# Mixers stage of a hybrid decoder step: scan output made feature by token

## The reference, cut to what matters

```python
cum = jnp.cumsum(dtc * a.reshape(g, r), axis=2)
seg = cum[:, :, :, None] - cum[:, :, None, :]
decay = jnp.exp(jnp.where(causal, seg, -jnp.inf))
cb = jnp.einsum('bcign,bcjgn->bcijg', cc, bc)
y_diag = jnp.einsum('bcijgr,bcjgrp->bcigrp', cb[..., None] * decay * dtc[:, :, None], xc)
to_end = jnp.exp(cum[:, :, -1:] - cum) * dtc
states = jnp.einsum('bcjgn,bcjgr,bcjgrp->bcgrpn', bc, to_end, xc)
# hc = exp(cum[-1]) * hc + states, chunk after chunk; h_prev is hc ahead of a chunk
y_off = jnp.einsum('bcign,bcigr,bcgrpn->bcigrp', cc, jnp.exp(cum), h_prev)
y = y_diag + y_off + xs * d_skip
y = y * silu(z)     # then a root-mean-square norm over each half of the features
```

## Time and profile before

| | |
|---|---|
| median of 3 runs | 1902.06 us (1902.06 to 1903.03) |
| the profiled execution | 1900.08 us, of which the span is 1898.1 |
| busy, share of the span | TensorE 96%, its weight loads 89%, VectorE 75%, ScalarE 47%, GpSimd 56% |
| mixers stage | about 797 to 1005 us of the span |

### The profile page before, as it was taken

How to read it: one execution, slowest core, us unless ns; L and a number is a source line. 1 busy time by engine, 2 the same in 40 slices (tenths; PEclk the granted TensorE clock), 3 DMA queues, 4 the chain that set the end, 5 groups by cost and what they waited for, 6 DMA issues and landing times.

```text
span 1898.1 us, 33584 instructions
## 1 busy us (share of the span) xinstructions
PE 1825.6 (96%) x12740; PEld 1686.7 (89%) x12740; DVE 1418.9 (75%) x1915; ACT 900.3 (47%) x1680; POOL 1066.2 (56%) x863
## 2 busy tenths in 40 slices
PE   8999999899999999999988999999999999999999
PEld 7999999888888889755557799999999998999999
DVE  5788840698888767589987564897777779787876
ACT  5334422677777778556642012343333344444442
POOL 4588740677756766334443222355555557787774
PEclk9999999999999999989999999999999999999999
DMA  4444442645455442789976524215334366434442
GB/s 175 149 156 176 183 148 75 159 117 124 101 134 120 125 124 90 253 304 322 321 244 214 190 97 186 91 45 205 147 125 165 148 230 254 159 137 147 148 136 92
DMA packets 139097, 309.31 MB, mean 163 GB/s; under 512 B 31659, under 2 KB 65323, under 8 KB 135228
## 3 DMA queue, kind: packets, MB, share of 16 engines
q1 hardware_dynamic: 115356, 271.15, 42.8%
q10 hardware_dynamic: 23584, 36.04, 5.6%
HBM read 222.42 MB, written 93.28 MB: 166 GB/s over the span
## 4 chain that ended last, share of the span: by engine, by line
PE 72%; DVE 13%; issue 6%; DMA 4%; ACT 3%; POOL 2%; SPq 0%; ACTq 0%; DVEq 0%; POOLq 0%
PE ff_ps L2742 32%; PE proj_ps L469 9%; PE dense_ps L1055 6%; PE wo_psa L2577 5%; PE proj_ps L552 3%; PE att_t_ps L1087 2%; PE wo_psb L2709 2%; DVE silu_half L1216 2%; DMA tmp_xbc<-silu_half 1%; PE wo_psa L2709 1%; PE att_s_ps L1073 1%; DVE att_p L1169 1%; PE att_s_ps L1074 1%; PE ssd_in L1773 1%; DVE sa_vlo L2108 1%
## 5 line engine op out<-in xcount | busy, mean ns | idle before, releaser
L2742 PE MATMUL ff_ps<-ff_set,ff_wring 128*128 128x264 f32 x5376 | 661.1, 285 | 11.1 <-DVE ff_set L3355 4.4
L2742 PEld LDWEIGHTS ff_ps<-ff_set,ff_wring 128*128 128x128 f32 x5376 | 658.0, 189 | 13.8 <-DVE ff_set L3355 5.3
L2411 POOL TENSOR_TENSOR ff_wring<-const,ff_wring 128x256 fp32r<-128x256 f32 (+1 forms) x192 | 211.9, 1107 | 148.0 <-ACT ff_wring L2908 147.9
L985 POOL TENSOR_SCALAR att_p<-att_p,att_rden 128x128 f32<-128x128 f32 (+6 forms) x112 | 197.0, 1768 | 117.1 <-DVE att_rden L1147 116.8
L2908 ACT ACTIVATE ff_wring<-const 128x256 fp32r<-128x256 f32 (+1 forms) x192 | 93.6, 489 | 220.4 <-PE ff_ps L2742 116.0
L3377 DVE TENSOR_TENSOR h<-h,ff_ps 128x528 f32<-128x528 f32 x192 | 133.2, 700 | 51.8 <-PE ff_ps L2742 47.2
L1282 ACT ACTIVATE att_pThi<-att_t_ps 128x512 fp32r<-128x512 f32 x192 | 93.2, 487 | 93.7 <-PE att_t_ps L1087 79.4
L1055 PE MATMUL dense_ps<-u_hi,w_hi 128*128 128x352 f32 x480 | 121.8, 335 | 4.7 <-POOL w_lo L254 2.1
L1169 DVE CUSTOM_DVE_ANT_0 att_p<-att_s_ps,att_bias 128x128 f32<-128x128 f32 (+7 forms) x128 | 94.9, 753 | 37.9 <-PE att_s_ps L1074 34.7
L1156 DVE TENSOR_TENSOR att_pTlo<-att_t_ps,att_pThi 128x512 fp32r<-128x512 f32 x192 | 104.5, 551 | 20.5 <-ACT att_pThi L1282 19.8
L1055 PE MATMUL dense_ps<-u_hi,w_lo 128*128 128x352 f32 x480 | 119.4, 330 | 0.0
(11 more groups left out here) (385 smaller groups left out, 4350.8 us busy)
## 6 DMA issues: line engine op xcount, KB each, us to landing
tmp_r_sets<-h SPq DMA_DIRECT2D x16, 1848.0 KB, 6.4
ff_setraw<-tmp_r_sets SPq DMA_DIRECT2D x56, 528.0 KB, 5.4
sa_k<-in_cache_k SPq DMA_DIRECT2D x32, 640.0 KB, 9.1
sa_v<-in_cache_v SPq DMA_DIRECT2D x40, 512.0 KB, 4.6
w_raw<-in_w_feat SPq DMA_DIRECT2D x36, 512.0 KB, 6.3
out_qk<-proj_out SPq DMA_DIRECT2D x16, 528.0 KB, 7.9
tmp_bias_rows<-tmp_table ACTq DMA_DIRECT2D x8, 1024.0 KB
att_bias<-tmp_bias_rows SPq DMA_DIRECT2D x16, 512.0 KB, 3.5
```

What stands on the lines that cost most here:

```text
L985: pool.tensor_scalar(slot(h, qt), slot(h, qt), rden[:, qt, :], None, ALU.mult).then_inc(normed, 1)
L2411: pool.tensor_tensor(w_set(n)[:, 1], operand(q, m), w_set(n)[:, 0].bitcast(F32), ALU.subtract).then_inc(fw_split, 1)
L2742: mm = pe.matmul(ff_ps[:, (b + g) * 512:(b + g) * 512 + HG], ws[:, wi, k, :], xs[:, xi, k, g * HG:(g + 1) * HG], start=(opens and k == 0 a ...
```

## The change

- `inner(n, g)` now makes y with features on partitions. For each pair of heads (f = 0 to 3, r = 0, 1) x of a head (64 columns) is the weights and `mixm` (128 columns) the data; r picks partitions 0 to 63 or 64 to 127 of the output. For n > 0 two more products add the state of the head (weights) times `grown` (data) in PSUM. `off`, `scale_off`, `add_inner`, `turn_y` and the two `y` buffers are gone; `add_skip` reads the new PSUM tiles `y_ps` (two banks) directly.
- `grown[g]` is exp(cum of the token) times C, for eight heads: `grow_exp(n, g)` on ScalarE makes the exponential from the rows in `mixm`, `grow(n, g)` on GpSimd multiplies by C.
- The decay of the state is `decay(n, 0)` and `decay(n, 1)` on GpSimd, each behind `inner(n, g)`.
- Order on TensorE for n > 0: scores 0 and 1, gather, scores 2 and 3, `inner(n, 0)`, `states(n, 0)`, `chunk_start(n+1)`, `sample_turn(n)`, `inner(n, 1)`, `states(n, 1)`, values.
- Order on ScalarE, VectorE, GpSimd and SP: as in the diff. The squares have their own tile `sq` instead of sharing `skipped`.

```diff
@@ tiles
+        sq = sb("ssd_sq", [P, KD, P])
+        misc_ps, in_odd_ps, t_ps = ps("ssd_misc", 512), ps("ssd_in1", 512), ps("sa_t", 512)
+        y_ps = in_ps, in_odd_ps
@@ load_chunk(n), and its place in the loop on SP
                 if n >= 2:
+                    sp.wait_ge(x_turned, 2 * (n - 1))
+                    sp.wait_ge(bcb_made, n - 1)
                     sp.wait_ge(skip_made, n - 1)
+                if n >= 3:
+                    sp.wait_ge(grown_made, 2 * (n - 2))
...
                 if n:
                     load_z(n)
+                if n + 2 < NC:
+                    load_chunk(n + 2)
                 if n + 1 < NC:
                     load_v(n + 1)
-                if n + 2 < NC:
-                    load_chunk(n + 2)
@@ inner(n, g)
-                if 2 * n + g:
-                    pe.wait_ge(y_summed, 2 * n + g)
-                for h in range(8 * g, 8 * g + 8):
-                    if h % 4 == 0:
-                        pe.wait_ge(mix_made, 4 * n + h // 4 + 1)
-                    mm = pe.matmul(in_ps[:, (h % 8) * HD:(h % 8 + 1) * HD], mixm[n % 2][:, h, :],
-                                   xdt[:, h * HD:(h + 1) * HD], start=True, stop=True)
+                if n:
+                    pe.wait_ge(y_skipped, 2 * n + g - 1)
+                    pe.wait_ge(grown_made, 2 * n + g - 1)
+                    pe.wait_ge(state_summed, 2 * n + g - 1)
+                for f in range(4):
+                    if f % 2 == 0:
+                        pe.wait_ge(mix_made, 4 * n + 2 * g + f // 2 + 1)
...
+                    for r in range(2):
+                        mm = pe.matmul(out(r), xdt[:, cols(r)], mixm[n % 2][:, 8 * g + 2 * f + r, :], start=True, stop=(n == 0))
+                    if n:
+                        for r in range(2):
+                            mm = pe.matmul(out(r), state[:, cols(r)], grown[g][:, 2 * f + r, :], start=False, stop=True)
                 mm.then_inc(in_made, 1)
@@ order on TensorE
             for n in range(NC):
                 if n:
-                    off(n, 0)
-                    turn_y(n - 1, 0)
                     sample_scores(n, 0)
-                    off(n, 1)
                     sample_scores(n, 1)
                     sample_gather(n - 1)
                     sample_scores(n, 2)
-                    turn_y(n - 1, 1)
                     sample_scores(n, 3)
-                states(n, 0)
-                inner(n, 0)
-                states(n, 1)
-                if n:
+                    inner(n, 0)
+                    states(n, 0)
+                    if n + 1 < NC:
+                        chunk_start(n + 1)
                     sample_turn(n)
-                inner(n, 1)
+                    inner(n, 1)
+                    states(n, 1)
+                else:
+                    states(n, 0)
+                    inner(n, 0)
+                    states(n, 1)
+                    inner(n, 1)
                 sample_values(n, 0)
@@ GpSimd
+            def grow(n, g):
+                pool.wait_ge(grown_exp, 2 * n + g - 1)
+                pool.wait_ge(loaded[n % 2], 16 * (n // 2 + 1))
+                pool.tensor_tensor(grown[g][:], grown[g][:],
+                                   xbc[n % 2][:, KD + 2 + g, :].unsqueeze(1).broadcast_to([P, NH // 2, P]),
+                                   ALU.mult).then_inc(grown_made, 1)
+
+            def decay(n, g):
+                pool.wait_ge(in_made, 2 * n + g + 1)
+                pool.wait_ge(state_summed, 2 * n + g - 1)
+                pool.tensor_tensor(heads(state[:, half(g)]), heads(state[:, half(g)]),
+                                   per_head(decays[:, 2, n, 8 * g:8 * g + 8]), ALU.mult).then_inc(state_decayed, 1)
...
                 if n:
+                    decay(n, 0)
                     new_bias(n)
-                    pool.wait_ge(off_made, 2 * n)
-                    pool.wait_ge(state_summed, 2 * n)
-                    pool.tensor_tensor(heads(state[:]), heads(state[:]), per_head(decays[:, 2, n, :]),
-                                       ALU.mult).then_inc(state_decayed, 1)
                 if n + 1 < NC:
                     place(n + 1)
-                    if n:
-                        sum_squares(n - 1)
+                if n:
+                    decay(n, 1)
+                    sum_squares(n - 1)
+                if n + 1 < NC:
+                    grow(n + 1, 0)
+                    skip_x(n + 1)
                     weigh_x(n + 1)
-                    skip_x(n)
+                    grow(n + 1, 1)
@@ ScalarE
+            def grow_exp(n, g):
+                act.wait_ge(rows_loaded[n % 2], 16 * (n // 2 + 1))
+                if n >= 2:
+                    act.wait_ge(in_made, 2 * n + g - 1)
+                act.activation(grown[g][:], mixm[n % 2][:, 8 * g:8 * g + 8, :], ACT.Exp).then_inc(grown_exp, 1)
+
+            def segment_next(n, q):
+                act.wait_ge(grown_exp, 2 * n + q // 2 - 1)
+                segment(n, q)
...
+                if n + 1 < NC:
+                    grow_exp(n + 1, 0)
+                    segment_next(n + 1, 0)
+                    segment_next(n + 1, 1)
                 if n:
                     exponent(n)
                     square(n - 1)
                     keep_probs(n)
                 spread_den(n)
                 if n + 1 < NC:
+                    keep_b(n + 1)
                     cast_v(n, 3)
-                    keep_b(n + 1)
                     cast_v(n, 4)
-                    for q in range(4):
-                        segment(n + 1, q)
+                    grow_exp(n + 1, 1)
+                    segment_next(n + 1, 2)
+                    segment_next(n + 1, 3)
@@ VectorE, the loop for n > 0
                     mix(n, 2)
-                    scale_off(n, 1)
-                    add_skip(n - 1, 0)
                     mix(n, 3)
-                    if n < NC - 1:
-                        split_v(n, 0)
-                        split_v(n, 1)
-                    add_skip(n - 1, 1)
+                    split_v(n, 0)
+                    split_v(n, 1)
+                    gate(n - 1)
                     softmax_min(n)
                     keep_out(n - 1)
...
+                    add_skip(n, 0)
+                    add_state(n, 0)
+                    invert(n)
+                    split_v(n, 2)
+                    split_probs(n)
+                    add_skip(n, 1)
+                    add_state(n, 1)
...
                 if n + 1 < NC:
+                    mask_cb(n + 1)
                     split_v(n, 3)
-                    mask_cb(n + 1)
                     weigh(n + 1, 0)
                     split_v(n, 4)
                     weigh(n + 1, 1)
                     keep_own(n)
-                    scale_off(n + 1, 0)
                     mix(n + 1, 0)
                     mix(n + 1, 1)
                     if n:
                         keep_norm(n - 1)
```

More of the change, by code:

```diff
@@ L2187, in _ @@
                         keep_norm(n - 1)
-            mixed.dve_tail = keep_own, add_skip, gate, keep_out, keep_norm, split_v
+            mixed.dve_tail = keep_own, gate, keep_out, keep_norm, split_v
     return mixed
@@ L2616, in _ @@
                 step(k, (0, 1))
-                if k == 0:
-                    turn_y(last, 1)
                 if k == 1:
@@ L3090, in scale @@
                                          op1=ALU.mult).then_inc(y_scaled, 1)
-            keep_own, add_skip, gate, keep_out, keep_norm, split_v = mixed.dve_tail
+            keep_own, gate, keep_out, keep_norm, split_v = mixed.dve_tail
             last = mixed.chunks - 1
```

123 lines of the change are left out of this document (36 added, 87 removed).

## The result

The changed kernel took 1940.69 us (median of 4 runs, 1933.61 to 1943.77) beside 1902.06 before: ratio 1.020, 95% interval 1.0182 to 1.0218. It is slower, as forecast, but by 38.6 us, not by 20.9, and it lies outside the range of 1899 to 1936.

A forecast was written before the change was run, and what follows sets the result against it. VectorE in order, TensorE in order and DMA were taken as close bounds of the 23.73 us chunk. Six periods of 29.0 (25.6 + 1.4 + 2.0) against 146.8, with -6.3, gave +20.9: 1923.0 us, range 1899 to 1936.

The forecast's parts named there:

- parts 3 and 4: ScalarE and GpSimd queues: `exponent` delayed to T + 6.7 (T: a chunk's last `sample_scores` out), TensorE idle 4.8 us.
- rival (c): In `inner`, the halves of TensorE's array don't overlap: 3.4 us each, period 32.4, time 1943 us; chance 0.06.
- Rival (b): On ScalarE, `exponent` isn't held and starts by T + 5.0; DMA decides at 22.3 us, time 1884; chance 0.09.
- The bare chain: Steady chunk, T to T, without lock or clock costs: 25.6 us; as a rival 1902.6 us, chance 0.13.
- The clock alone: TensorE at 1.2 GHz after its stand in each chunk: 2.0 us lost, range 0 to 3.
- The lock alone: VectorE and GpSimd wait for each other's whole instruction at the shared port: 1.4 us a chunk, range 0 to 3.3.
- Together -6.3: First and last chunks of the mixers stage: 2.6 us gained at the start and 3.7 at the end.
- the start: Chunk 0 and the scores of chunk 1: T comes 2.6 us earlier.
- the dead heat: After `inner(n, 1)`, `grow` is ready in 3.1 us, `split_v(n, 3)` in 3.05; `grow` first costs 3.3 us, otherwise 1.4.
- Part 1: TensorE: two `off` products and two `turn_y` removed, `inner` at 1.7 us; 3.2 us less work per chunk.
- the tail: Chunk 7: values end at T + 17 instead of T + 20.7, 3.7 us kept.
- (d): Steady chunk with longer half clock and the lock lost each time: period 31.9 us, time 1940 us; chance 0.06.

The follow-up runs named there:

- filled_twice: `filled` plus two filling products ahead of the scores of each chunk from the second on: 1916.34 us, ratio 1.0074.
- filled_short: The changed kernel with five filling products ahead of `sample_turn` and `grow` cut to one head of eight: 1917.89 us, ratio 1.0091.
- late_exponent: `early_pieces_gate` with ScalarE in the changed kernel's order again, `grow_exp` and two quarters of segments ahead of `exponent`: 1918.67 us, ratio 1.0072.
- short_grow: The changed kernel with `grow` cut to one head of eight, the product with C left out for the others: 1934.49 us, ratio 1.0177.
- pieces: The changed kernel with `grow`, `skip_x` and `weigh_x` on GpSimd each issued as four instructions: 1930.94 us, ratio 1.016.
- bias_first: The changed kernel with `new_bias(n)` ahead of `decay(n, 0)` on GpSimd: 1938.24 us, ratio 1.0197.
- filled: The changed kernel with five filling products on TensorE ahead of `sample_turn`, all other order kept: 1922.52 us, ratio 1.0114.
- tail_pieces: `early_pieces_gate` with the low parts of the first four weights made in four instructions each on GpSimd: 1885.71 us, ratio 0.9898.
- early_pieces_gate: The changed kernel with bias a chunk earlier, exponent first on ScalarE, GpSimd's long products in four pieces, gate behind `add_state(n, 0)`: 1890.53 us, ratio 0.9936.
- early_gate: `early_pieces_gate` with GpSimd's products whole again, or the gate ahead of the softmax again on VectorE (the latter is this run): 1908.31 us, ratio 1.0022.

## Why the prediction was right in kind and wrong in size

- **The stand** (parts 3 and 4): forecast `exponent` at T + 6.7 and 4.8 us of stand, found T + 6.8 to 6.9 and 4.60 to 4.75 us (3.6 in chunk 7). `inner` 1.7 to issue and 1.95 until its result is told forecast, 1.85 and 2.0 found (GpSimd and ScalarE start behind it at T + 2.0; in the chunk shown the rows of `cum` landed 0.15 us later still). The halves of the array do run side by side: rival (c) falls. Rival (b), the exponent not held, falls too.
- **The bare chain**: 25.6 forecast, 25.8 by `filled_twice`, 25.6 by one chunk of `filled_short`. Right.
- **The clock alone**: 2.0 forecast; `late_exponent` has 27.5 with neither lock wait nor second stretch, which leaves 1.7. Right, though the price moves with the work that the stretch falls on: the chunk of `short_grow` at 887.47, without a second stretch too, has 28.3.
- **The lock alone**: 1.4 forecast; 0.8 at full clock in `filled_twice`. Right in kind. The Trainium skill (SBUF — State Buffer, section "SBUF: two separate sides") states the port as an exclusive lock held for a whole instruction; the rows of 878.79 and 910.14 above agree, in both directions (GpSimd's 2.39 becomes 3.41 when it loses).
- **What failed, in the forecast's own terms.** By the spans the change came 23.0 us above the forecast (43.9 against 20.9): 11.3 in "Period: 25.6 + 1.4 + 2.0 = 29.0", 10.7 in "Together -6.3" for start and end, and 1.1 outside the stage. The mean period of 30.88 lies within the forecast's 26.6 to 31; with the start and end as forecast it would have given 1934, inside the range. So two steps failed: the sum of the period, and the 6.3 us taken for start and end, in which lock and clock stood at nothing.
- **The first failed step, the sum of lock and clock.** The two terms are not independent. Alone they make 25.8 + 1.7 + 0.8 = 28.3; together the chunk took 30.88, so 2.6 us a period, some 15 us in six, belong to neither. The rows show two ways. First, the half clock shifts the dead heat: at full clock the split won by 0.04 us in the chunk shown, and in the periods of 31.3 the half clock reaches into `states(n, 1)` (869.22 to 876.05), values and with them cast and split come later, while GpSimd's queue, released by `inner(n, 1)`, does not, and `grow` wins by 0.2. Second, the waits that the lock adds to TensorE are followed by a second stretch of half clock, 3.4 us long (882.87 and 917.01). I had priced one drop a chunk and found two. In the periods of 30.0 the second one explains most of the excess: TensorE is busy for 3.03 us in it at half rate, by estimate 1.5 us lost on top of 28.3.
- **How far the lock's part in the second drop is shown.** All six periods of the changed kernel have a lock wait of 0.77 to 2.36 us and a second stretch; `pieces` and `late_exponent`, with no such wait in their steady chunks, have none; `short_grow` has both kinds of chunk, 28.3 twice with waits of at most 0.4 us and no second stretch, and 31.3 with a wait of 1.95 us and one. But the wait's length doesn't settle it: in the first period of `short_grow` 0.45 us was followed by a second stretch, and 0.8 us doesn't bring it every time: the last periods of `bias_first` and `short_grow` have one and no second stretch (28.6 and 28.5, about the 28.3 of the plain sum), and in `filled`, without any stand, it came in two chunks of six.
- **A sign that was in the trace before.** I took the price of the clock from the one gap of over 3 us. But in chunk 1 the kernel before runs some 10 us at half clock behind waits of 0.90 us (825.36 in the earlier trace rows) and 1.39 us (its timeline, and the stretch):

```profile
831.45 1.48 PE L1762 MATMUL ssd_off<-ssd_xw,ssd_btok 128*128 128x512 f32 x2 [1.39 <-DVE ssd_state L2067]
...
832.10:842.40 10.30, 10.30 (x41) 7.98 (x40) 6.42 (x10) 3.38 (x7) 1.99 (x2) 0.50 0.53 173
```

  So short waits could bring a drop, and the 146.8 us hold one period of 28.45 beside five of 23.4 to 23.7: against a steady chunk the change costs 7.2 us, not the 6.4 of the mean periods.
- **A cover that I took away without a price.** In the shorter periods the second drop (917.01) follows the 1.43 us of TensorE ahead of the scores. In the kernel before, TensorE had work there, an `off` and a turn, and in its steady periods it waits no longer than 1.0 us anywhere (its timeline, and its longest wait over five periods):

```profile
893.88 1.02 PE L1751 MATMUL ssd_off<-ssd_state,ssd_xbc 128*128 128x512 f32 x2
894.74 0.60 PE L1733 MATMUL ssd_yturn<-const,ssd_y 128*128 128x128 f32 x4
...
PE ssd_off L1762 <- DVE ssd_state L2067: 4.6, 5, 1.0
```

  Part 1 booked both as relief. Off the chain, they had covered the wait for `keep_own`. That gap alone brings no drop (`late_exponent` has it in every chunk); 1.1 us behind the lock's wait of 0.77 us it was followed by one in both such chunks, and `filled_twice`, which puts work there again, has periods of 26.6 where `filled` still has some of 28.
- **The second failed step, the start**: forecast -2.6, found +1.1. I had priced the lock only in the steady chunk. In chunk 0 a split is held behind `grow` (2.92 us) and another behind `skip_x` (2.47), and TensorE waits 2.70 us at the turn of x. With the same products in pieces, `pieces` has 31.2 us from the first turn of x to T of chunk 1, 2.4 less than before: the forecast's gain was there and the lock took it.
- **The same step, the tail**: forecast -3.7, found +3.3 (+3.7 to the end of the values, where the forecast had set its mark), from the lock against the first weights (3.36 us for a split, 4.10 us of TensorE's wait) and 13.7 us of half clock where the kernel before had 10.2. Even `tail_pieces`, with the lock eased, is only 1.6 us shorter there than the kernel before, so some 2 us of the 3.7 are still missing, part of them in the wait of 2.37 us shown above. "What follows is in order on VectorE" counted what had moved away and not what came next in that queue.
- **The rest**: +1.1 us lies outside the stage. The profiled run is also 3.1 us above the median of its kernel.
- **The rivals**: (d), lock lost and longer half clock, named the right pair and the right time, 1940, at a chance of 0.06. It was treated as two mishaps at once, each unlikely; the rows above link them. That its time fits is in part luck: its period of 31.9 is 1 us too long, and it kept the 6.3 us at start and end. The range, too, ended at a period of 31 with these 6.3 us gained in full.
- **The change with its queues mended** is 1.0% under the kernel before. In the chunk of 892.60 TensorE is busy 19.29 us and VectorE 19.77, 3.2 and 1.6 less than in the earlier trace rows, and the period is 23.2. What sets it there isn't shown: DMA is at 0.94, but TensorE stands for the exponent too, and the chain that ended last (880 to 940 us) goes for about half over ScalarE's segments, casts and exponentials. Nor is it shown that the 1.0% is all the change's: no run gave the kernel before the same mending, and the pieces of `skip_x`, `weigh_x` and the weights could help it as well.

## What to carry to other kernels

Before moving an instruction on one queue, list what the critical instruction behind it waits for on every queue; here one exponential and two quarters of segments ahead of a softmax, and the place of the bias on GpSimd, cost more than the arithmetic saved. Don't add the price of a stall and the price of a lock as if they were independent: a stall that lowers TensorE's clock shifts the races behind it, and a lock's wait can be followed by another drop, so give the case in which both happen a chance of its own, and price both at the start and in the tail too. Work moved to GpSimd beside a busy VectorE is cheaper in several short instructions than in one long one (11 us here), if nothing that is waited for stands behind them: in `pieces` the bias did, and the stand grew.

## What the runs showed of the hardware

- A product of GpSimd over 1,024 elements with two full inputs takes 2.39 us undisturbed and up to 3.46 (`bias_first`) when it begins just behind a split of VectorE; a split of 1.2 us takes up to 3.47 behind it. I had expected the second, not that the loser is so often GpSimd.
- Such a product in four pieces takes 0.72 us for a piece by itself, but 3.8 to 5.9 us for the four in `pieces` and `tail_pieces`, beside VectorE's work, and none of the splits in four steady chunks of `early_pieces_gate` takes longer than 1.63 us. With whole products (`early_gate`) they take up to 3.22.
- Half clock came with the stands of 4.6 us, 6.8 us at a time; and 3.4 us of it came behind a wait of 2.36 us, and behind waits of 0.77 and 1.43 us, 1.1 us apart. The last pair was followed by a drop in both of its chunks in the changed kernel and in two of six in `filled`, where no stretch had gone before. In the kernel before, waits of 0.90 and 1.39 us in chunk 1 were followed by some 10 us of half clock and waits of at most 1.0 us in the steady chunks by none; in `tail_pieces` waits of 1.4 and 1.5 us in each chunk were followed by none either. The length of a single wait does not decide it.
